# Moving the causal-conv steps and the SiLUs within the differential-attention loop of a one-core transformer block

## The reference, cut to what matters

```python
def one_block(args):
    q_blk, start = args
    s = jnp.einsum('bhmqd,bhmkd->bhmqk', q_blk, k).astype(jnp.float32)
    q_pos = start + jnp.arange(Q_BLOCK)
    causal = k_pos[None, :] <= q_pos[:, None]
    p = jax.nn.softmax(jnp.where(causal, s, -jnp.inf), axis=-1)
    a = p[:, :, 0] - lam * p[:, :, 1]
    return jnp.einsum('bhqk,bhkd->bhqd', a.astype(v.dtype), v)
...
y_da = diff_attention(...)
qk = jax.nn.silu(causal_depthwise_conv(jnp.concatenate([mq, mk], axis=-1), ml_conv_w, ml_conv_b))
mq_c, mk_c = jnp.split(qk, 2, axis=-1)
y_ml = mlstm_chunkwise(mq_c, mk_c, mv, mo, ...)
```

## Time and profile before

| | |
|---|---|
| median of 3 runs | 1479.91 us (1479.79, 1479.91, 1482.86) |
| profiled execution, its own time | 1482.86 us |
| its span (first to last instruction) | 1481.0 us |
| TensorE busy in the span | 1339.9 us (90%) |
| VectorE, ScalarE, GpSimd busy | 538.2, 414.5, 389.1 us (36%, 28%, 26%) |
| mean granted TensorE clock | 0.970 of full speed |

### The profile page before, as it was taken

The page is one execution under the profiler, slowest core; times in us unless marked ns, Lnnn a source line. Parts: engine busy times, 40 slices in busy tenths (PEclk is TensorE's granted clock), DMA queues, the critical chain, the costliest instruction groups (busy, mean ns, idle before and its releaser), DMA issues. The chain is left out here.

```text
span 1481.0 us, 16780 instructions
## 1 busy us (share of the span) xinstructions
PE 1339.9 (90%) x6344; PEld 892.0 (60%) x6344; DVE 538.2 (36%) x1074; ACT 414.5 (28%) x810; POOL 389.1 (26%) x372
## 2 busy tenths in 40 slices
PE   7999998999999799888888788866999999999799
PEld 6777766898758633333222223325888887788467
DVE  3649947430242511111111111127321414563753
ACT  5333365163331100000000000024223224343641
POOL 7553223168320112111111111100445440000321
PEclk9999988999999899999999999998999999999999
DMA  7221221244205879999999999983222322222000
GB/s 210 74 98 58 93 79 45 102 167 142 85 5 212 366 310 420 420 424 420 424 422 421 423 423 421 423 318 136 96 104 85 114 86 85 86 86 86 29 22 36
DMA packets 72368, 298.27 MB, mean 201 GB/s; under 512 B 10168, under 2 KB 10216, under 8 KB 51568
## 3 DMA queue, kind: packets, MB, share of 16 engines
q1 hardware_dynamic: 64848, 282.80, 48.7%
q0 software_dynamic: 7456, 14.59, 3.1%
HBM read 293.16 MB, written 12.58 MB: 206 GB/s over the span
## 5 line engine op out<-in xcount | busy, mean ns | idle before, releaser
L748 POOL TENSOR_TENSOR ring_rounded<-ring,ring_rounded 128x512 fp32r<-128x512 f32 x192 | 251.5, 1346 | 350.0 <-ACT ring_rounded L1463 350.0
L875 PE MATMUL bank<-HT_rounded,ring_rounded 128*128 128x512 f32 (+1 forms) x576 | 220.9, 383 | 4.4 <-DVE ring_rounded L2358 3.5
L877 PE MATMUL bank<-HT_rounded,ring_rounded 128*128 128x512 f32 (+1 forms) x576 | 217.5, 378 | 0.0
L876 PE MATMUL bank<-ring_rounded 128*128 128x512 f32 (+1 forms) x576 | 217.4, 377 | 0.0
L1176 PE MATMUL bank<-ring,B 128*64 128x512 f32 x704 | 170.3, 633 | 43.2 <-DMA ring<-in_w 42.3
L2250 DVE TENSOR_TENSOR B<-bank,small 128x512 f32<-128x512 f32 x32 | 22.1, 692 | 325.4 <-PE bank L1166 325.4
L1176 PEld LDWEIGHTS bank<-ring,B 128*64 128x64 f32 x704 | 52.1, 144 | 145.3 <-issue 105.0
L877 PE MATMUL bank<-ring_rounded 128*128 128x512 f32 x352 | 137.7, 391 | 0.0
L1463 ACT ACTIVATE ring_rounded<-ring 128x2048 fp32r<-128x2048 f32 x54 | 102.8, 1915 | 108.8 <-DMA ring<-in_w_in_a 46.3
L875 PEld LDWEIGHTS bank<-HT_rounded,ring_rounded 128*128 128x128 f32 x576 | 108.3, 188 | 31.1 <-issue 6.0
L876 PEld LDWEIGHTS bank<-ring_rounded 128*128 128x128 f32 x576 | 108.4, 188 | 20.3 <-issue 1.0
(11 more groups left out here) (382 smaller groups left out, 1988.1 us busy)
## 6 DMA issues: line engine op xcount, KB each, us to landing
ring<-in_w SPq DMA_DIRECT2D x88, 1024.0 KB, 30.2
A<-in_w SPq DMA_DIRECT2D x21, 2048.0 KB, 28.6
ring<-in_w SPq DMA_DIRECT2D x11, 2048.0 KB, 28.6
XN<-in_w SPq DMA_DIRECT2D x20, 1024.0 KB, 29.1
HT<-in_w SPq DMA_DIRECT2D x20, 1024.0 KB, 32.2
ring<-in_w_in_a SPq DMA_DIRECT2D x16, 1024.0 KB, 5.0
ring<-in_w_in SPq DMA_DIRECT2D x14, 1024.0 KB, 7.0
ring<-in_w_in_b SPq DMA_DIRECT2D x8, 1024.0 KB, 5.3
```

The costliest lines, as they stand in the source:

```text
L748: last = pool.tensor_tensor(r32(lo), lo, r32_read(quarter(g, True)[:, k, :]), ALU.subtract)
L875: pe.matmul(o, r32(a_hi), r32(b_hi), start=first, stop=False)
L876: pe.matmul(o, r32(a_hi), r32(b_lo), start=False, stop=False)
L877: return pe.matmul(o, r32(a_lo), r32(b_hi), start=False, stop=last)
```

## The change

The table CONV_AT goes. It said in which VectorE iteration each of the eight convs stands: 1, 2, 3, 5, 6, 7, 9 and 10. Now conv j follows the weighting of step j, which puts them in iterations 1 to 8. ScalarE's SiLUs stand in iteration 11 instead of 13.

```diff
-CONV_AT = {1: 0, 2: 1, 3: 2, 5: 3, 6: 4, 7: 5, 9: 6, 10: 7}
...
-                if i == 13:
+                if i == 11:
                     act.wait_ge(sem("conv_done"), 8)
                     for m in range(8):
                         act.activation(mqkT[:, m, :], mqkT[:, m, :], ACT.Silu).then_inc(sem("silu_ready"), 1)
...
-                    if i in CONV_AT:
-                        conv(CONV_AT[i])
+                    if j < 8:
+                        conv(j)
```

## The result

The kernel after took 1489.03 us (median of 7 runs, 1487.00 to 1491.67), the kernel before on the same chip 1480.90 (7 runs, 1479.71 to 1485.21). The ratio is 1.0051, 95% interval 1.0035 to 1.0067: **slower by 7.5 us (5.2 to 9.9)**. The forecast was 1482.2 with a range up to 1484.9, so it was wrong, in size and in the line that it drew around "no change". Run again later (e9) against 31 runs of before it came to 1.0035 (1.0020 to 1.0049), 5.2 us (3.0 to 7.3). Both intervals lie above the forecast of 2.3.

The account below looks back on a forecast made before the run. TensorE was taken to bound the attention loop. One stall of 2.3 us, all other terms 0, on the median of 1479.91 gave 1482.2 us; range 1480.0 to 1484.9.

Parts of the forecast that it names:

- The bound and the link: Attention loop: TensorE bounds it; tightest link is its `do` matmuls waiting for VectorE's copy, slack 4.38 us in iteration 5.
- (a): Iteration 4: conv(3) beside GpSimd takes 6.6 us, its copy is late, and TensorE stalls 2.3 us in iteration 5.
- (b): Iteration 5: conv(4) replaces conv(3), copy done at 144.7, TensorE asks at 145.6; no second stall.
- (c): Iterations 6 and 7 keep their length with conv(5), conv(6); VectorE about 2 us late, TensorE 2.3.
- (d): Iteration 8: conv(7) and copies end 165.3 to 166.4, TensorE asks at 167.3; no stall, 0 to 0.1 if all held up.
- (e): Iterations 9 and 10 lose their conv; nobody waited there, so it brings nothing.
- (f): SiLUs moved from iteration 13 to 11: 0 us, up to 0.3 if the handoff is slow.
- (g): Loop's end, where TensorE waits 2.14 us for VectorE: moves as a whole and gives nothing back.
- Rival D: First heads' scores after the loop: half clock avoided, twice 2.1 us won, 2.3 lost, total 1478.0; chance 0.07.
- Rival B: TensorE's clock falls to 1.2 GHz behind the stall in the loop, costing 1.7 us more, total 1483.9; chance 0.27.
- E: Loop stalls in iterations 6, 9 and at the SiLUs add up: 3.4 us, 1483.3, or 1485.0 with clock fall; chance 0.12.

Follow-up runs that it names:

- e9: Kernel after unchanged, measured again against before; ratio 1.0035, 5.2 us over.
- e5: Kernel after, but GpSimd starts the low part of the mv chunk only when conv 4 is done; ratio to before 1.0058, 8.6 us over.
- e2: Kernel before with only the SiLUs moved to iteration 11, convs where they were; ratio to before 1.0004, 0.6 us over.
- e8: Kernel before with nine dummy TensorE matmuls (about 4 us) in iteration 5, no wait; ratio to before 1.0029, 4.3 us over.
- e1: Kernel after with the SiLUs back in iteration 13, so only the convs are moved; ratio to before 1.0035, 5.2 us over.
- e12: Kernel before with only conv 3 moved from iteration 5 to 4, measured again beside the kernel after; ratio to before 1.0048.
- e3: Kernel before with only conv 3 moved from VectorE's iteration 5 to 4; ratio to before 1.0035, 5.2 us over.
- e6: Kernel after with five dummy TensorE matmuls (about 2.2 us) ahead of its wait in iteration 5; ratio to before 1.0038, 5.6 us over.
- e11: Kernel after with two GpSimd stretches moved behind convs: mv chunk waits for conv 4, mo chunk for conv 7; ratio to before 1.0000.
- e10: Kernel before with only conv 6 moved from iteration 9 to 8; ratio to before 0.9991, -1.3 us.

## Why the prediction was wrong, step by step

- **The bound and the link: right.** TensorE was the bound, and the copy of iteration 4 the one link that broke.
- **(a) The stall: the mechanism right, one size in two missed.** 2.3 was forecast and 2.26 and 2.29 came in two profiles, but 3.20, 3.35 and 3.33 in three. I counted the hold-ups from the conv on and took VectorE's scaling ahead of it as fixed. In the trace of before GpSimd's start (129.08) lay right beside that scaling, which showed no hold-up, and I did not ask what 0.1 us of drift would do:

```profile
129.00 0.48 DVE L1957 TENSOR_SCALAR E<-E,small 128x512 f32<-128x512 f32 x1
```

  The upper bound should have had another 0.9. That the first profile had 2.26 is luck as much as counting.
- **(b), (c), (d): right.** No second wait. In (d) the second stretch was counted from 160.2 and began at 162.30, so one step of the conv was held up where the working had three or four. That the first wait moves this stretch was in the working, and e5 shows how much hangs on it: 6 us of wait.
- **(e), (f): right.** e2: nothing that could be told.
- **(g): right for the loop's end, not shown for the rest.** The wait at the end stayed (2.13). "Gives nothing back" fits e8's 4.3 us, but in the profiles the mLSTM stage did give back 3.1 of 4.2 us by the clock, and later stages took as much and more. Rival D had this as a case of its own, at 0.07; it didn't make the kernel faster.
- **The choice among the rivals is the step that failed.** The forecast put the clock's fall at nothing. I took the clock as kept because one wait of 3.26 had not brought it down, against one of 1.69 that had the earlier trace rows. Here it fell in four of five profiles with this wait idle (after, e1, e9, e12; not e3). Rival B, at 0.27, was the case in the loop. Its price of 1.7 is measured as 1.7 to 1.8. The trace of before had more to go by. The wait of 2.14 at the loop's end, nearly the size of the forecast one, is followed by the half clock that I used for rival D only. From 95 us on its timeline has 14 waits of TensorE over 2 us, and the clock was below full within 3 us behind nine of them (six of the ten waits up to 2.5 us). And the wait of 3.26 that spoke for a kept clock stands in six of the fourteen profiles; in the five others (after, e1, e5, e6, e11) the clock fell. Forecast and rival B added up over the five profiles give 4.3 us for the loop (4.03, 4.98, 2.51, 5.08, 5.02), nearly twice the forecast.
- **The scale.** I set the sum on a median of three runs, with a range 4.9 us wide, where single runs of before spread by 8 or more. Outside the loop the fourteen profiles spread by 7.7. No rival reached the first comparison's 5.2 to 9.9 either: B stood 4.0 over before, E with a fall 5.1.
- **Open:** the five comparisons of kernels with this wait left idle give 5.2, 5.2, 5.2, 7.1 and 7.5 us, 6.0 on average, where the loops give 4.3 on average. Three of the intervals reach down to 4.3, two don't (4.7 and 5.2). Whether a late loop loses 1 to 2 us more in later stages wasn't settled; e8, late by 3.92 without a wait, lost 4.3, with an interval too wide to say, and e5, late by 9.36, lost 8.6. Nor is it settled how the loop's 4.3 us come through the mLSTM stage, where the profiles give most of it back, to the end. That the time hangs on the meeting of conv 3 and GpSimd is shown by the runs (e3 and e12 against e11); how the microseconds add up behind the loop is not.

## What to carry to other kernels

When work is moved on one engine, look at which of its neighbours on other engines it will stand beside, not only at what it delays: here 2.8 us of conv became 6.5 because its new place lay in GpSimd's stretch, and only the slot's slack (4.38 or 6.15) decided whether this was a loss. Where two engines' starts lie within 0.2 us of each other in the trace, count both outcomes. And a pause of over 2 us in a stretch that TensorE bounds should be priced with the clock's fall as the likelier case: count all waits of that size in the trace at hand, not one for each side. Filling the pause with dummy work kept the clock up in the one profile that tried it.

## What was not expected of the hardware

The prices of the hold-up were in the rows of before, and the runs repeat them: beside GpSimd a VectorE step of two inputs from SBUF takes 1.6 to 1.7 us instead of 0.75, a tensor_scalar 1.4 to 1.5 instead of 0.5, while copies out of PSUM keep their 0.55. Not expected was that GpSimd's stretch grows too, from 10.95 to 12.05 or so under four such steps more, and how fine the line is: the same tensor_scalar is held up in full with GpSimd's start 0.01 us behind its own (e10), and not at all with 0.08 (before). And the program's time outside the loop moves by 7.7 us from one profile to the next, as much as the largest effect measured for this change.
